# Layer boundaries of a ten-layer float32 kernel: norms in halves, low parts and transposes in another order

## The chip, the cores and the metric

One core of one Trainium2 chip. The metric is device time in microseconds of one execution. TensorE (PE in the rows) does matmuls and transposes, VectorE (DVE) and ScalarE (ACT) do elementwise work, GpSimd (POOL) small roots and masks, SyncE (SP) issues the loads.

## What is computed

256 tokens of width 1024, all in float32. First one block: a SwiGLU layer, a hybrid mixer of three attention kinds, a SwiGLU layer, each with `x = layer_norm(alpha * x + f * layer(x))`. Then a second block with pre-norm residual layers, `x = x + layer(rmsnorm(x, g))`: SwiGLU, a short convolution, SwiGLU, then keys and values that later layers share, SwiGLU, sparse attention (NSA), SwiGLU. The kernel calls these ten layers phases 0 to 9: FFN, MIXER, FFN, FFN, CONV, FFN, KV, FFN, NSA, FFN. The norms between them are

```python
layer_norm: (xf - mu) * rsqrt(var + 1e-5) * g + b
rmsnorm:    xf * rsqrt(mean(xf * xf) + 1e-6) * g
```

Boundary n is what lies between phase n and phase n + 1. Boundaries 0 and 1 have a LayerNorm, boundary 2 a LayerNorm and then an RMS norm, 3 to 8 an RMS norm alone. Boundary 5 leads into KV; the norm of boundary 6 is computed inside KV, which adds nothing to x.

## The kernel before

**Weights** arrive as slabs of 128 x 2048 floats, some narrower (`raw`, six slots), in the order in which they are used. SyncE loads slab k when slab k - 6 is used (`slab_used`). ScalarE rounds a slab to its high part (`split`, L646, `w_hi`), VectorE subtracts to get the low part (`split`, L1016, `w_lo`); `split_to(k)` on either engine does all slabs up to k that are not done. A product is three groups of matmuls: high x high and activation-low x weight-high, which need `w_hi`, and activation-high x weight-low, which needs `w_lo`. Activations are split in the same way.

**Input of a phase.** The 256 tokens are two tiles (`tt` = 0, 1) of 128. When a tile is normed, TensorE turns it (`transpose_input`, L1601) by two quarters of four 128 x 128 transposes, ScalarE copies a quarter out (`xT_hi`, L660), VectorE subtracts the low part (`xT_lo`, L1030). `next_input(n, tt)` on TensorE waits for the norm of a tile and turns both quarters. The operand is x_sb for phases 1 and 2 and z_sb (the RMS norm's output) from phase 3 on.

**End of a phase.** `project` does the last matrix slab by slab into four PSUM banks, one for each tile and half of 512 columns. The last three slabs (four at boundary 2, `tail`) are done for tile 0 first and then for tile 1, so that tile 0's output is complete (`y_ready`) while tile 1's slabs run. Each slab and tile is one `part`: four matmuls of 128 x 512 in each of three groups (L1626, L1629, L1633). `next_input(n + 1, 0)` stands ahead of the last part of tile 1.

**Start of a phase.** In `by_token` the first four slabs (two in phase 0, three in KV) are done for tile 0, then for tile 1; `next_input(n, 1)` stands ahead of slab 2 after an RMS norm alone and ahead of slab 3 after a LayerNorm. `token_slab` (L1694, L1697, L1700) does one slab's three groups.

**The norm, engine by engine.** VectorE's `boundary` adds the output to x in two halves of 512 columns (L1046, L1049). For a LayerNorm it takes the statistics (L1056 to L1059), waits for GpSimd's power of -0.5 (`root`, L590), subtracts the mean and multiplies by the gain (L1067), multiplies by the root and adds the bias (L1069). For an RMS norm ScalarE squares the row of 1024 and sums it (`norm`, L671), VectorE scales and adds epsilon (L1074), GpSimd takes the root, VectorE multiplies by root and gain (L1078). Then the turned input is evacuated (`evacuate_input`).

**Order of the work around the norm.** VectorE: low parts up to slab 2 of the next phase (slab 1 at boundary 2), tile 0's norm and copy; tile 1's addition; then low parts up to slab 3 between its steps (after the LayerNorm's statistics, where boundary 2 stops at slab 2 and does slab 3 ahead of the RMS norm; without a LayerNorm right after the addition), its norm and copy. ScalarE: high parts up to slab 2 (1), tile 0's square and copy, high parts up to slab 3, tile 1's square and copy. Each engine works strictly in the order written by hand; all waits are on semaphores.

In KV, VectorE runs low parts, small clears, the two RMS norms of the next phase's input, a norm of keys and then `xc_lo` (L1359), which the matmuls of L2027 wait for.

## Time and profile before

| | us |
|---|---|
| median of three runs | 1700.6 (1693.1 to 1703.9) |
| the profiled execution, its own time | 1695.3 |
| span of its instructions | 1693.5 |
| TensorE busy | 1647.3 (97%) |
| VectorE busy | 1027.8 (61%) |
| ScalarE busy | 804.6 (48%) |

Loads bring 291 MB at 172 GB/s on average. The span runs from the first to the last instruction of the profiled execution; its own time holds what lies around it, 1.8 us. Busy is the union of an engine's instruction spans; a matmul's end is modelled and spans overlap, so busy TensorE is not TensorE at its peak. The "granted clock" is the share of TensorE's full clock that it was given.

### The profile page before, as it was taken

The page shows a single profiled execution, that of the slowest core. Times are in us where ns is not written, and L with a number is a line of the kernel's source. Part 1 is how long each engine was busy: PE and PEld are TensorE (multiplying, and loading weights), DVE is VectorE, ACT ScalarE, POOL GpSimd, SP SyncE. Part 2 cuts the span into 40 slices and gives each one's busy share as a digit, 9 for nine tenths or more (in the row PEclk, how much of TensorE's full clock was granted, in tenths as well). Part 3 has the DMA queues.
Part 4 walks back from the last instruction along what each step waited for, and adds up shares of the span by engine and source line. Part 5 has one row for each costly group of instructions (what it writes and reads, how often), then busy time and mean ns, then how long its engine had stood idle before and what let it go on. Part 6 is the DMA issues. An engine that isn't in the chain of part 4 may idle for free.

```text
span 1693.5 us, 21209 instructions
## 1 busy us (share of the span) xinstructions
PE 1647.3 (97%) x8854; PEld 1413.7 (83%) x8854; DVE 1027.8 (61%) x1172; ACT 804.6 (48%) x1066; POOL 32.6 (2%) x53
## 2 busy tenths in 40 slices
PE   8999999998999998999999999999999989999998
PEld 6888898866788887888898888889888877888887
DVE  5666565866756656665557566567666444556662
ACT  5555344655355533455334455456455333545551
POOL 0000000000000000000000000000000020000000
PEclk9999999989999999999999999999999986999999
DMA  8565474423556645665565565557565540037552
GB/s 275 179 220 199 137 261 137 137 93 118 174 187 186 236 149 174 199 200 187 173 211 169 180 198 197 190 194 219 174 206 182 172 167 1 2 120 223 184 195 75
DMA packets 226096, 291.23 MB, mean 172 GB/s; under 512 B 10516, under 2 KB 203728, under 8 KB 225872
## 3 DMA queue, kind: packets, MB, share of 16 engines
q1 hardware_dynamic: 226000, 289.87, 52.4%
q8 instruction: 70, 1.15, 0.3%
q14 instruction: 26, 0.21, 0.0%
HBM read 288.78 MB, written 1.05 MB: 171 GB/s over the span
## 4 chain that ended last, share of the span: by engine, by line
PE 84%; DVE 8%; ACT 3%; issue 2%; DMA 2%; POOL 1%; SPq 0%; DVEq 0%; POOLq 0%; ACTq 0%
PE bank L1771 22%; PE bank L1776 12%; PE bank L1626 6%; PE bank L1633 6%; PE bank L1629 6%; PE bank L1694 5%; PE bank L1697 5%; PE bank L1700 5%; DVE w_lo L1016 2%; PE bank L1668 2%; PE bank L1670 2%; PE bank L1675 2%; PE bank L2087 2%; PE bank L1601 1%; PE bank L2112 1%
## 5 line engine op out<-in xcount | busy, mean ns | idle before, releaser
L1016 DVE TENSOR_TENSOR w_lo<-raw,w_hi 128x2048 fp32r<-128x2048 f32 (+1 forms) x268 | 602.4, 2271 | 197.4 <-ACT w_hi L646 196.4
L646 ACT ACTIVATE w_hi<-raw 128x2048 fp32r<-128x2048 f32 (+1 forms) x268 | 508.8, 1904 | 187.3 <-DMA raw<-in_ffn_w_down_dram 92.9
L1771 PE MATMUL bank<-xT,w_hi 128*128 128x512 f32 x1664 | 397.3, 391 | 0.0
L1771 PEld LDWEIGHTS bank<-xT,w_hi 128*128 128x128 f32 x1664 | 306.1, 188 | 59.6
L1776 PEld LDWEIGHTS bank<-xT,w_lo 128*128 128x128 f32 x1664 | 213.3, 191 | 8.1
L1776 PE MATMUL bank<-xT,w_lo 128*128 128x256 f32 x1664 | 215.9, 283 | 0.0
L963 ACT ACTIVATE silu<-bank 128x256 f32<-128x256 f32 x104 | 34.2, 381 | 215.6 <-PE bank L1776 215.6
L1626 PE MATMUL bank<-w_hi,hT_hi 128*128 128x512 f32 x528 | 134.2, 390 | 0.0
L1629 PE MATMUL bank<-w_hi,hT_lo 128*128 128x512 f32 x528 | 133.5, 389 | 0.0
L1633 PE MATMUL bank<-w_lo,hT_hi 128*128 128x512 f32 x528 | 133.5, 389 | 0.0
L1694 PE MATMUL bank<-w_hi,xT 128*128 128x512 f32 (+2 forms) x464 | 126.2, 404 | 6.7 <-ACT w_hi L646 4.0
L1697 PE MATMUL bank<-w_hi,xT 128*128 128x512 f32 (+2 forms) x464 | 119.4, 388 | 0.0
L1700 PE MATMUL bank<-w_lo,xT 128*128 128x512 f32 (+2 forms) x464 | 118.5, 386 | 0.0
L1629 PEld LDWEIGHTS bank<-w_hi,hT_lo 128*128 128x128 f32 x528 | 99.1, 188 | 20.7
L1633 PEld LDWEIGHTS bank<-w_lo,hT_hi 128*128 128x128 f32 x528 | 99.1, 188 | 20.6
L1626 PEld LDWEIGHTS bank<-w_hi,hT_hi 128*128 128x128 f32 x528 | 98.4, 188 | 19.9
L1694 PEld LDWEIGHTS bank<-w_hi,xT 128*128 128x128 f32 x464 | 87.0, 196 | 25.1 <-issue 6.1
L1697 PEld LDWEIGHTS bank<-w_hi,xT 128*128 128x128 f32 x464 | 87.2, 190 | 17.8
L1700 PEld LDWEIGHTS bank<-w_lo,xT 128*128 128x128 f32 x464 | 86.7, 189 | 17.3
L1540 DVE TENSOR_TENSOR h<-silu,h 128x512 f32<-128x512 f32 x52 | 36.0, 693 | 96.4 <-ACT silu L969 96.4
L1535 DVE TENSOR_TENSOR silu<-bank,silu 128x256 f32<-128x256 f32 x104 | 39.3, 419 | 70.7 <-ACT silu L963 70.7
L1668 PE MATMUL bank<-xT,w_hi 128*128 128x256 f32 x304 | 76.0, 289 | 0.0
(268 smaller groups left out, 1592.4 us busy)
## 6 DMA issues: line engine op xcount, KB each, us to landing
raw<-in_ffn_w_gate_up_dram SPq DMA_DIRECT2D x176, 512.0 KB, 4.8
raw<-in_ffn_w_down_dram SPq DMA_DIRECT2D x132, 512.0 KB, 4.1
raw<-in_ffn_w_gate_dram SPq DMA_DIRECT2D x44, 512.0 KB, 4.0
raw<-in_ffn_w_up_dram SPq DMA_DIRECT2D x44, 512.0 KB, 5.1
raw<-in_w_in_dram SPq DMA_DIRECT2D x44, 512.0 KB, 4.9
raw<-in_conv_w_in_dram SPq DMA_DIRECT2D x24, 512.0 KB, 4.7
raw<-in_kv_w_dram SPq DMA_DIRECT2D x12, 512.0 KB, 4.4
raw<-in_w_out_dram SPq DMA_DIRECT2D x8, 512.0 KB, 3.9
```

The lines of the kernel that those rows point to most:

```text
L646: nc.scalar.activation(w_hi[:, slot, 0:width], raw[:, slot, 0:width], ACT.Copy).then_inc(high_ready, 1)
L1016: nc.vector.tensor_tensor(w_lo[:, slot, 0:width], raw[:, slot, 0:width], w_hi[:, slot, 0:width].bitcast(F32), ALU.subtract).then_inc(low_r ...
L1535: ins = nc.vector.tensor_tensor(part[:, fb % 2, :], FEATURES[j % 2][fb][:, 0:S], part[:, fb % 2, :], ALU.add)
L1626: nc.tensor.matmul(o, lhs_hi[:, 2 * d + c, toks], hi[:, c, at], start=d == 0 and c == 0, stop=False, skip_group_check=True)
L1629: nc.tensor.matmul(o, lhs_lo[:, 2 * d + c, toks], hi[:, c, at], start=False, stop=False, skip_group_check=True)
L1633: ins = nc.tensor.matmul(o, lhs_hi[:, 2 * d + c, toks], lo[:, c, at], start=False, stop=d == slabs - 1 and c == 1, skip_group_check=True)
L1668: nc.tensor.matmul(o, hi[:, c, at], xT_hi[:, 4 * kh + c, :], start=kh == 0 and c == 0 and fb % 2 == 0, stop=False, skip_group_check=True)
L1694: nc.tensor.matmul(dst(tt), xT_hi[:, 4 * kh + c, toks], hi[:, c, at], start=kh == 0 and c == 0 and not (shared and tt), stop=False, skip_g ...
L1697: nc.tensor.matmul(dst(tt), xT_lo[:, 4 * kh + c, toks], hi[:, c, at], start=False, stop=False, skip_group_check=True)
L1700: ins = nc.tensor.matmul(dst(tt), xT_hi[:, 4 * kh + c, toks], lo[:, c, at], start=False, stop=kh == 1 and c == 3, skip_group_check=True)
L1771: nc.tensor.matmul(o[:], hi[:, c, at], x, start=kh == 0 and c == 0, stop=False, skip_group_check=True)
L1776: ins = nc.tensor.matmul(o[:, 0:S], lo[:, c, at], xT_hi[:, 4 * kh + c, :], start=False, stop=kh == 1 and c == 3, skip_group_check=True)
```

## The change

- `row_half` and `input_half` are new semaphores. They tell that the first 512 columns of a tile of x are added (or layer-normed), and that the first 512 columns of the next input are ready.
- ScalarE squares each tile in two halves with two sums, the first as soon as `row_half` allows; VectorE combines the sums with one more small operation.
- VectorE applies a LayerNorm's centring before it waits for the root, and its scaling in two halves; the RMS norm's product too is in two halves.
- VectorE's low parts: before tile 0's norm up to slab 2 at boundaries 0 and 1, else up to slab 1. None between tile 1's addition and the end of its norm. Behind the norm and ahead of tile 1's copy: slab 3 at boundaries 0 and 1, slab 2 at 3, 4, 5, 7, 8, none at boundary 2; the rest up to slab 3 behind the copy.
- ScalarE's high part of slab 3 moves from ahead of tile 1's square to behind it where there is no LayerNorm.
- TensorE turns quarter by quarter, each behind its own wait. `next_input(n + 1, 0)` moves from ahead of the last part of tile 1 into it, behind six of its twelve matmuls.
- Phase 3 (behind boundary 2) has its own order: for tile 0 slabs 0 and 1, then the two groups of slabs 2 and 3 that need only high parts, with tile 1's transposes between the last two groups; the same for tile 1 with the hidden layer's transposes (`hidden(0)`) between; then the low groups of slabs 2 and 3 for both tiles.

The diff, cut to what the text speaks of:

```diff
                     for tt in tiles:
-                        if has_ln(n):
-                            act.wait_ge(normed, normed_at(n, tt, LN))
-                        else:
-                            act.wait_ge(summed, summed_before(n) + (tt + 1 if kind != KV else 0))
-                        nc.scalar.activation(z_sb[:, tt, :], x_sb[:, tt, :], ACT.Square,
-                                             accum_out=stats[:, 8 + tt:9 + tt]).then_inc(squared, 1)
+                        for half in range(2):
+                            if phases[n] == KV:
+                                act.wait_ge(summed, summed_before(n))
+                            elif half == 0:
+                                act.wait_ge(row_half, rows_before[n] + tt + 1)
+                            elif has_ln(n):
+                                act.wait_ge(normed, normed_at(n, tt, LN))
+                            else:
+                                act.wait_ge(summed, summed_before(n) + tt + 1)
+                            at, total = slice(half * 512, (half + 1) * 512), (8, 14)[half] + tt
+                            nc.scalar.activation(z_sb[:, tt, at], x_sb[:, tt, at], ACT.Square,
+                                                 accum_out=stats[:, total:total + 1]).then_inc(squared, 1)
...
                         norm(n, [tt])
+                        if tt == 1:
+                            split_to(first_slab[n + 1] + 3)
                         evacuate_input(inputs_before(n + 1), TOKENS_FIRST[2 * tt:2 * tt + 2], 2 * tt)
-                        if tt == 0:
+                        if tt == 0 and has_ln(n):
                             split_to(first_slab[n + 1] + 3)
...
+                        if half == 0 and has_rms(n):
+                            ins.then_inc(row_half, 1)
...
                 xt, mean, rstd = x_sb[:, tt, :], stats[:, 4 * tt:4 * tt + 1], stats[:, 4 * tt + 3:4 * tt + 4]
-                dve.wait_ge(rstd_ready, normed_at(n, tt, LN))
                 dve.wait_ge(gain_loaded[0], 16 * (ln_uses[n] + 1))
...
                                                     op0=ALU.subtract, op1=ALU.mult))
-                nc.vector.scalar_tensor_tensor(out=xt, in0=xt, scalar=rstd, in1=gain[:, 1, :],
-                                               op0=ALU.mult, op1=ALU.add).then_inc(normed, 1)
+                dve.wait_ge(rstd_ready, normed_at(n, tt, LN))
+                first_half = row_half if has_rms(n) else input_half
+                for half, done in enumerate((first_half, normed)):
+                    at = slice(half * 512, (half + 1) * 512)
+                    nc.vector.scalar_tensor_tensor(out=x_sb[:, tt, at], in0=x_sb[:, tt, at], scalar=rstd, in1=gain[:, 1, at],
+                                                   op0=ALU.mult, op1=ALU.add).then_inc(done, 1)
             def rms_norm(n, tt):
-                dve.wait_ge(squared, NT * rms_uses[n] + tt + 1)
-                nc.vector.tensor_scalar(stats[:, 10 + 2 * tt:11 + 2 * tt], stats[:, 8 + tt:9 + tt], 1.0 / D, RMS_EPS,
-                                        ALU.mult, ALU.add).then_inc(spread, 1)
+                mean = stats[:, 10 + 2 * tt:11 + 2 * tt]
+                for half in range(2):
+                    dve.wait_ge(squared, 2 * (NT * rms_uses[n] + tt) + half + 1)
+                    if half == 0:
+                        step(nc.vector.tensor_scalar(mean, stats[:, 8 + tt:9 + tt], 1.0 / D, RMS_EPS, ALU.mult, ALU.add))
+                    else:
+                        nc.vector.scalar_tensor_tensor(out=mean, in0=stats[:, 14 + tt:15 + tt], scalar=1.0 / D, in1=mean,
+                                                       op0=ALU.mult, op1=ALU.add).then_inc(spread, 1)
                 dve.wait_ge(rstd_ready, normed_at(n, tt, RMS))
                 dve.wait_ge(gain_loaded[2], 16 * (rms_uses[n] + 1))
-                nc.vector.scalar_tensor_tensor(out=z_sb[:, tt, :], in0=x_sb[:, tt, :], scalar=stats[:, 11 + 2 * tt:12 + 2 * tt],
-                                               in1=gain[:, 2, :], op0=ALU.mult, op1=ALU.mult).then_inc(normed, 1)
+                for half, done in enumerate((input_half, normed)):
+                    at = slice(half * 512, (half + 1) * 512)
+                    nc.vector.scalar_tensor_tensor(out=z_sb[:, tt, at], in0=x_sb[:, tt, at], scalar=stats[:, 11 + 2 * tt:12 + 2 * tt],
+                                                   in1=gain[:, 2, at], op0=ALU.mult, op1=ALU.mult).then_inc(done, 1)
             def boundary(n, factor, y_at):
-                split_to(first_slab[n + 1] + 5 - tail(n))
+                split_to(first_slab[n + 1] + (2 if has_ln(n) and not has_rms(n) else 1))
                 for tt in range(NT):
...
                         layer_norm(n, tt, factor)
-                        if tt == 1:
-                            split_to(first_slab[n + 1] + (2 if has_rms(n) else 3))
                         layer_norm_apply(n, tt)
+                    if has_rms(n):
+                        rms_norm(n, tt)
+                    if tt == 1 and not (has_ln(n) and has_rms(n)):
+                        split_to(first_slab[n + 1] + (3 if has_ln(n) else 2))
+                    if n < last:
+                        evacuate_input(inputs_before(n + 1), TOKENS_FIRST[2 * tt:2 * tt + 2], 2 * tt)
                     if tt == 1:
                         split_to(first_slab[n + 1] + 3)
-                    if has_rms(n):
-                        rms_norm(n, tt)
-                    if n < last:
-                        evacuate_input(inputs_before(n + 1), TOKENS_FIRST[2 * tt:2 * tt + 2], 2 * tt)
...
                 else:
+                    pe.wait_ge(input_half, NT * (n - 1) + tt + 1)
+                transpose_input(operand(n), TOKENS_FIRST[2 * tt:2 * tt + 1])
+                if n > 0:
                     pe.wait_ge(normed, normed_at(n - 1, tt))
-                transpose_input(operand(n), TOKENS_FIRST[2 * tt:2 * tt + 2])
+                transpose_input(operand(n), TOKENS_FIRST[2 * tt + 1:2 * tt + 2])
...
                                          skip_group_check=True)
-                    for c, toks, at, o in each:
+                    for i, (c, toks, at, o) in enumerate(each):
+                        if between and i == len(each) // 2:
+                            between()
                         nc.tensor.matmul(o, lhs_lo[:, 2 * d + c, toks], hi[:, c, at], start=False, stop=False, skip_group_check=True)
...
+                        between = None
...
-                            next_input(n + 1, 0)
-                        ins = part(d, [tt], tt == 1)
+                            between = lambda: next_input(n + 1, 0)
+                        ins = part(d, [tt], tt == 1, between)
...
+                if between:
+                    between()
...
+            def slab_low(k, kh, width, at, dst, tiles=range(NT)):
...
+                hi, lo = slab_view(k % SLOTS, 4, width)
...
-                for c, tt, toks in each:
-                    ins = nc.tensor.matmul(dst(tt), xT_hi[:, 4 * kh + c, toks], lo[:, c, at], start=False, stop=kh == 1 and c == 3,
-                                           skip_group_check=True)
+                for c in range(4):
+                    for tt in tiles:
+                        ins = nc.tensor.matmul(dst(tt), xT_hi[:, 4 * kh + c, tt * P:(tt + 1) * P], lo[:, c, at], start=False,
+                                               stop=kh == 1 and c == 3, skip_group_check=True)
...
+            def token_slab(k, kh, width, at, dst, shared=False, tiles=range(NT)):
...
+                slab_high(k, kh, width, at, dst, shared, tiles)
+                return slab_low(k, kh, width, at, dst, tiles)
...
                         tile(1)
+                    elif has_ln(n - 1) and has_rms(n - 1):
+                        def high(kh, tt, between=None):
+                            slab_high(s0 + 2 + kh, kh, 512, slice(0, 512), lambda tt: bank[2 + tt][:], tiles=[tt], between=between)
+
+                        for tt in range(NT):
+                            for kh in range(2):
+                                pe.wait_ge(xT_ready, 4 * inputs_before(n) + 2 * tt + kh + 1)
+                                gate_up(0, kh, [tt])
+                            high(0, tt)
+                            if tt == 0:
+                                high(1, 0, lambda: next_input(n, 1))
+                            else:
+                                hidden(0)
+                                high(1, 1)
+                        for kh in range(2):
+                            slab_low(s0 + 2 + kh, kh, 512, slice(0, 512), lambda tt: bank[2 + tt][:]).then_inc(slab_used, 1)
                     else:
```

## Rows read from the trace of the kernel before

**Rows 1.** The page: each engine's busy time.

```profile
PE 1647.3 (97%) x8854; PEld 1413.7 (83%) x8854; DVE 1027.8 (61%) x1172; ACT 804.6 (48%) x1066; POOL 32.6 (2%) x53
```

**Rows 2.** Waits of the whole span, transposes: us, times, longest us.

```profile
PE bank L1601 <- DVE z_sb L1078: 8.9, 12, 4.4
```

**Rows 3.** The groups by line: busy us, mean ns, idle us before.

```profile
L1601 PE MATMUL bank<-ident,x_sb 128*128 128x128 f32 x48 | 7.9, 322 | 7.7 <-DMA x_sb<-in_x_dram 4.3 <-DVE x_sb L1069 3.4
```

**Rows 4.** Timeline, boundary 1, first token tile: start us, duration us, engine.

```profile
451.40 0.55 POOL L590 TENSOR_TENSOR stats<-stats,minus_half 128x1 f32<-128x1 f32 x1 [241.92 <-DVE stats L1059]
...
451.98 1.28 DVE L1067 SCALAR_TENSOR_TENSOR x_sb<-x_sb,stats,gain 128x1024 f32<-128x1024 f32 x1 [0.67 <-POOL stats L590]
...
453.30 1.28 DVE L1069 SCALAR_TENSOR_TENSOR x_sb<-x_sb,stats,gain 128x1024 f32<-128x1024 f32 x1
...
454.64 1.09 PE L1601 MATMUL bank<-ident,x_sb 128*128 128x128 f32 x8 [1.88 <-DVE x_sb L1069]
...
455.97 1.29 DVE L1030 TENSOR_TENSOR xT<-bank,xT 128x512 fp32r<-128x512 f32 x2 [1.38 <-ACT xT L660]
...
458.34 1.07 PE L1694 MATMUL bank<-w_hi,xT 128*128 128x512 f32 x4
```

**Rows 5.** The timeline, boundary 2 (LayerNorm and RMS norm), second token tile.

```profile
645.12 1.07 PE L1694 MATMUL bank<-w_hi,xT 128*128 128x512 f32 x4
...
648.28 2.28 DVE L1016 TENSOR_TENSOR w_lo<-raw,w_hi 128x2048 fp32r<-128x2048 f32 x1
648.44 2.53 POOL L590 TENSOR_TENSOR stats<-stats,minus_half 128x1 f32<-128x1 f32 x1 [8.38 <-DVE stats L1059]
...
653.52 2.29 DVE L1016 TENSOR_TENSOR w_lo<-raw,w_hi 128x2048 fp32r<-128x2048 f32 x1
...
654.61 0.19 ACT L671 ACTIVATION_READ_ACCUMULATOR z_sb<-x_sb 128x1 f32 x1
...
657.88 1.97 PE L1601 MATMUL bank<-ident,z_sb 128*128 128x128 f32 x8 [4.43 <-DVE z_sb L1078]
...
659.50 2.05 PE L1694 MATMUL bank<-w_hi,xT 128*128 128x512 f32 x4
...
663.91 1.07 PE L1694 MATMUL bank<-w_hi,xT 128*128 128x512 f32 x4
```

**Rows 6.** Windows of boundaries 1 and 2: five engines busy us, then granted clock.

```profile
452.00:468.00 16.00, 13.89 (x69) 11.17 (x68) 11.54 (x13) 3.31 (x4) 2.54 (x1) 1.00 0.59 192
658.00:661.00 3.00, 3.00 (x12) 2.71 (x13) 1.18 (x2) 1.72 (x3) 0.00 (x0) 0.50 0.02 5
```

**Rows 7.** The timeline, boundary 4 (convolution to feed-forward), both token tiles.

```profile
924.74 1.06 ACT L671 ACTIVATE z_sb<-x_sb 128x1024 f32<-128x1024 f32 x1 [3.56 <-DVE x_sb L1049]
...
928.08 1.09 PE L1601 MATMUL bank<-ident,z_sb 128*128 128x128 f32 x8 [0.86 <-DVE z_sb L1078]
...
933.17 2.28 DVE L1016 TENSOR_TENSOR w_lo<-raw,w_hi 128x2048 fp32r<-128x2048 f32 x1
...
937.52 1.09 PE L1601 MATMUL bank<-ident,z_sb 128*128 128x128 f32 x8 [0.16 <-DVE z_sb L1078]
```

**Rows 8.** The timeline: transposes on TensorE that waited for nothing.

```profile
1485.53 1.07 PE L1633 MATMUL bank<-w_lo,xT 128*128 128x512 f32 x4
...
1486.44 1.03 PE L1601 MATMUL bank<-ident,z_sb 128*128 128x128 f32 x8
...
1487.23 1.17 PE L1626 MATMUL bank<-w_hi,xT 128*128 128x512 f32 x4
...
1490.05 1.07 PE L1626 MATMUL bank<-w_hi,xT 128*128 128x512 f32 x4
```

**Rows 9.** The timeline of the shared keys' layer, VectorE and then TensorE.

```profile
1142.17 6.69 DVE L1016 TENSOR_TENSOR w_lo<-raw,w_hi 128x2048 fp32r<-128x2048 f32 x3
1149.12 5.72 DVE L1359 TENSOR_TENSOR xc_lo<-bank,xc_hi 64x512 fp32r<-64x512 f32 x8 [0.27 <-ACT xc_hi L863]
...
1152.70 0.39 PE L2027 MATMUL bank<-w_hi,xc_hi 128*80 128x256 f32 x1
```

7 lines of the change are left out of this document (5 added, 2 removed).

## Prediction

> **What bounds the kernel now.** I read the page first. TensorE is busy for 1647.3 of 1693.5 us, VectorE for 61% and ScalarE for 48% [rows 1]: the time is TensorE's own work plus what it waits for. So I then read the waits and the groups by line for the transposes that the change moves (L1601). They follow a norm, and TensorE stood idle before them for 8.9 us in 12 waits where they read z_sb [rows 2] and for 3.4 us where they read x_sb (the 4.3 us behind the load of x are the program's start) [rows 3]. These are two waits at each of eight boundaries (0 to 5, 7, 8), 16 in all, 12.3 us together; boundary 6 lies inside the shared-key layer and has none. Last the timelines. At boundary 1 the chain is statistics, GpSimd's root, centring (L1067), scaling (L1069), transposes, and TensorE has nothing else to do for 1.88 us [rows 4]. At boundary 2 a second norm follows, low parts of weights (L1016) stand between its steps, and TensorE waits 4.43 us [rows 5]. In that wait its granted clock fell: 0.50 in the window from 658 to 661 us, which is the 1.2 GHz level, against 1.00 (2.4 GHz) around boundary 1 [rows 6].
>
> **What the waits cost in all.** (a) Idle: 12.3 us. (b) A matmul group's span overlaps the next group: where transposes waited for nothing they began 0.91 us after the start of the group before, whose span is 1.07 us [rows 8]. A wait loses this overlap too: 0.16 us x 16 = 2.6 us. (c) From eight transposes to the end of the twelve matmuls behind them it took 1490.05 - 1486.44 = 3.61 us without a wait [rows 8] and 458.34 - 454.64 = 3.70 us with one [rows 4]: 0.09 x 16 = 1.4 us. (d) At the low clock the same work at boundary 2 took 663.91 - 657.88 = 6.03 us [rows 5] instead of 3.70: 2.3 us. Sum 18.6 us: the most that can be had.
>
> **Edit 1, transposes of the first tile inside the last slab.** TensorE now has six more matmuls ahead of the wait: 6 x 0.227 (0.91 us for four) = 1.4 us. Behind the transposes six remain to cover the copy of the turned input. L1030 starts 455.97 - 454.64 = 1.33 us behind the first transpose and its first half takes 0.65 [rows 4], so the next layer can begin at 2.0 to 2.1 us; transposes take 0.79 us and six of the twelve matmuls behind them half of 2.82 [rows 8], 2.2 us together. The cover holds by 0.1 to 0.2 us. If it is missed, it costs that much at eight boundaries, about 1 us.
>
> **Edit 2, norms by halves.** Scaling in halves lets the first four transposes start after 0.65 us instead of 1.28. The squares: ScalarE's 1.06 us plus 0.19 for reading the sum [rows 5, 7] become two of about 0.6 + 0.19, the first under the second half of the addition, so the sum is ready about 0.5 us earlier; VectorE gets one more small operation per tile (no row has its own length; 0.1 to 0.3, I take 0.2 with its step). An RMS norm is thus ready 1.1 us earlier. With the 1.4 us of edit 1, all first-tile waits of 0.2 to 1.9 us go. Second-tile waits outside boundary 2 are short, [rows 7] shows one of 0.16 us; there a whole low part (2.28 us) stood beside the square and ended about 1 us after it, and it goes too. These waits end.
>
> **Edit 3, centring before the root is awaited.** Before, the low part L1016 ran beside GpSimd's root and the root took 2.53 us instead of 0.55, ending at 650.97, 0.41 us after the low part [rows 4, 5]. Now the centring, also with two operands in SBUF, runs beside it. Between no conflict (scaling at once behind the centring's 1.28 us, 0.67 us won) and the same conflict (0.41 us later, 0.2 us won) I take the conflict, the nearest row. It matters only where the chain is late, at boundary 2: 0.4 us.
> The Trainium skill, SBUF — State Buffer, section Who interferes with whom, says that a VectorE instruction with two SBUF inputs holds up a GpSimd instruction that reads SBUF until it is finished. By it the conflict is certain and speaks against this edit; without it the sum would be 0.4 us better.
>
> **Boundary 2, second tile.** Count from S, the start of the next layer's first matmul (645.12 before). The root began at S + 3.32 [rows 5]; the addition and statistics ahead of it now end at S + 3.45 (0.2 later than before, since the copy of the first tile is still on VectorE); centring to 4.75, root to 5.2, first half scaled 5.85, second 6.5, second square with its sum 7.45, last statistic 7.7, root 8.35, first half of z 9.05. TensorE is there after two slabs, eight matmuls and four: 36 x 0.227 = 8.2. It waits 1.0 us instead of 4.6. Then three low parts stand ahead of the product that tile 0 of the hidden layer needs (slabs 2, 3 and 4, 2.23 us each in a row [rows 9]): they end about 9.5 us behind the transposes, the product 0.75 later at 10.25, while TensorE, with 4 + 24 + 8 matmuls, asks for it at 9.4: 0.85 us of new wait. With 0.15 for the second half of the transposes, 2.0 us remain here.
>
> **Edit 4, low parts leave the norm.** At boundaries 3, 4, 5, 7, 8 the low parts of slabs 2 and 3 now follow the second tile's norm. From S: z done at 4.9, slab 2's low part to 7.15, the turned copy to 8.4, slab 3's to 10.7. TensorE needs that at 5.44 + 0.79 + 2.82 + 1.81 = 10.86: covered, by 0.15 us. In the convolution and the NSA layer VectorE is idle soon after. In the shared-key layer it isn't. VectorE runs almost without a pause until L1359, whose fourth of eight pieces (5.72 / 2 = 2.86) ends at 1151.98, and TensorE needs it at 1152.70 [rows 9]: 0.72 us of slack. The moved low part brings 2.2 us to this chain, two extra small operations 0.4, the idle 0.27 absorbs some, and TensorE arrives 0.4 earlier for the waits it has lost: 2.2 + 0.4 - 0.27 + 0.4 - 0.72 = 2.0, with its overlap 2.1 us of new wait. Bounds: 0 (if slack I don't see absorbs it) and 2.6. At boundaries 0 and 1 one low part moves behind the norm, ahead of a copy that comes 3 us later: nothing.
> Each load (SyncE) waits for the same slab to be used as before; slabs 2 and 3 of layer 3 are released in the same order, none later. ScalarE's high part of slab 3 moves behind the second square, 9 us ahead of need. Nothing.
>
> **The sum.** 18.6 - 2.0 - 2.1 = 14.5 us. The profiled execution took 1695.3 us, so it would take 1680.8; the median of the runs shown is 1700.6, 0.3% above it, and the forecast is 1700.6 - 14.5 = 1686 us, 0.86% faster. A measurement of this kernel can tell about 1% from no change, so this counts as within 1%.
>
> **Rivals.**
> A, more comes: VectorE has hidden slack in the shared-key layer and in layer 3, no new wait arises: 1700.6 - 18.6 = 1682 us. For it: several short gaps of VectorE there. Against: the chain of [rows 9], with only 0.27 us of waiting ahead of L1359.
> B, the new waits throw the clock down: two waits of about 2 us (shared keys) and 1.0 and 0.85 us close together (boundary 2), each at the price of (d): 14.5 - 4.6 = 9.9, 1691 us. For it: 4.43 us did so. Against: 1.88 us at boundary 1 did not.
> C, the change doesn't bring what it says: TensorE arrives earlier and waits for weights instead (arrival or high part), since loads start only as slabs are released: 1700 us. Against: TensorE shows hardly any wait for w_hi, and VectorE and ScalarE have 39% and 52% free.
> D, slower: the low parts behind the norm come late. The mechanism: slabs 2 and 3 are both converted in the last 6 us before their use at boundaries 3, 4, 5, 7, 8; if both were exposed, 4.5 us each, with the clock falling as at boundary 2 (2.3 us), 5 x 6.8 = 34 us, less 14.5: 1720 us. It decides from the point where slab 3's low part comes about 2.9 us too late (5 x 2.9 = 14.5); I have it 0.15 us early. Against: that needs an error of a whole low part in my count.
>
> **Numbers.** Forecast 0.50 (its own range 1683 to 1689), A 0.25, B 0.12, C 0.09, D 0.04. Range 1679 to 1692: from the whole 18.6 us with 3 us of scatter to B's price; it leaves out C and D and the outer ends. Faster by over 1% is below 1683.6: most of A (0.19) and the lower tail of the forecast (0.12), 0.31; slower by over 1%: D, 0.04; within 1%: 0.65.
>
> **What would show it.** Idle before L1601 under 2 us in all; at boundary 2 one wait near 1.0 us for z and one near 0.85 for h, no fall of the granted clock; the root after LayerNorm near 1.6 us, ending 0.4 us behind the centring; in the shared-key layer a wait of about 2 us before the matmuls on xc. Wrong if the first slab behind each boundary waits for the turned copy, if slab 3's third group waits for w_lo, or if waits for w_hi appear.

## The result, and the profile after

The changed kernel took 1679.24 us (median of 4 runs, 1678.27 to 1681.10), the kernel before in the same comparison 1697.47 us (4 runs, 1693.1 to 1703.9). The ratio is 0.990, with an interval of 0.988 to 0.993. A second comparison, in five rounds, gave 1680.84 against 1696.81 us: 0.992 (0.990 to 0.994). The forecast was 1686 us, a ratio of 0.991, in a range of 1679 to 1692; the first median lies 0.24 us above the range's low end. The profiled execution took 1678.59 us with a span of 1676.9, against 1695.26 and 1693.5: 16.6 us less in the span.

The page of the changed kernel, each engine's busy time; it answers to [rows 1]:

```profile
PE 1642.5 (98%) x8854; PEld 1412.5 (84%) x8854; DVE 1031.0 (61%) x1206; ACT 806.0 (48%) x1094; POOL 34.7 (2%) x53
```

TensorE has the same 8854 matmuls. VectorE has 34 instructions more and ScalarE 28, for 3.2 and 1.4 us more of busy time: halves cost little on engines that are not the bound.

The waits of the changed kernel (us in all, times, longest); the third row answers to [rows 2]:

```profile
PE bank L1625 <- DMA x_sb<-in_x_dram: 4.3, 1, 4.3
...
PE bank L2085 <- DVE xc_lo L1383: 1.6, 1, 1.6
...
PE bank L1625 <- DVE z_sb L1102: 0.6, 1, 0.6
...
PE bank L1801 <- DVE h L1581: 0.4, 1, 0.4
```

Line numbers have moved: the transposes are L1625 (before L1601), the low parts L1028 (L1016), the low part of the shared keys' columns L1383 (L1359) and its user L2085 (L2027). The first row is the load of x at the program's start, as before. Of the 12 waits for z_sb, 8.9 us, one of 0.6 us is left; the group for x_sb shows none on a norm at all, where [rows 3] had 3.4 us. The last row (the hidden layer's product) and the second (the shared keys) are new waits, both foretold.

Boundary 1, first token tile, of the changed kernel; it answers to [rows 4]. Timeline: start us, duration us, engine. PEld is the weight load, which for a transpose is what waits first:

```profile
446.18 1.28 DVE L1080 SCALAR_TENSOR_TENSOR x_sb<-x_sb,stats,gain 128x1024 f32<-128x1024 f32 x1
446.33 1.54 POOL L594 TENSOR_TENSOR stats<-stats,minus_half 128x1 f32<-128x1 f32 x1 [240.10 <-DVE stats L1073]
...
447.99 1.42 DVE L1086 SCALAR_TENSOR_TENSOR x_sb<-x_sb,stats,gain 128x512 f32<-128x512 f32 x2 [0.52 <-POOL stats L594]
...
448.44 0.62 PE L1658 MATMUL bank<-w_hi,xT 128*128 128x512 f32 x2
448.79 0.46 PEld L1625 LDWEIGHTS bank<-ident,x_sb 128*128 128x128 f32 x4 [0.16 <-DVE x_sb L1086]
448.90 1.22 PE L1625 MATMUL bank<-ident,x_sb 128*128 128x128 f32 x8
449.45 0.42 PEld L1625 LDWEIGHTS bank<-ident,x_sb 128*128 128x128 f32 x4 [0.20 <-DVE x_sb L1086]
...
450.16 1.31 DVE L1042 TENSOR_TENSOR xT<-bank,xT 128x512 fp32r<-128x512 f32 x2 [0.76 <-ACT xT L664]
...
450.41 1.09 PE L1662 MATMUL bank<-w_lo,xT 128*128 128x512 f32 x4
...
451.33 1.07 PE L1724 MATMUL bank<-w_hi,xT 128*128 128x512 f32 x4
```

The root now begins with the centring and takes 1.54 us instead of 0.55. The scaling is one row of two pieces, and the transposes start 0.91 us after its start; in [rows 4] it was 1.34 us. TensorE works up to 449.06, so its row shows no wait; only the weight loads waited 0.16 and 0.20 us. The six matmuls behind the transposes reach to the next layer's first matmul (L1724), which has no wait either: the cover of the first tile's copy held, here and at the other seven boundaries.

Boundary 2, second token tile; it answers to [rows 5], with S = 635.88 (the first L1724 of the layer):

```profile
635.88 1.07 PE L1724 MATMUL bank<-w_hi,xT 128*128 128x512 f32 x4
...
639.21 1.55 POOL L594 TENSOR_TENSOR stats<-stats,minus_half 128x1 f32<-128x1 f32 x1 [7.06 <-DVE stats L1073]
...
643.13 1.07 PE L1724 MATMUL bank<-w_hi,xT 128*128 128x512 f32 x4
...
643.98 1.41 DVE L1102 SCALAR_TENSOR_TENSOR z_sb<-x_sb,stats,gain 128x512 f32<-128x512 f32 x2 [0.66 <-POOL stats L594]
...
644.79 1.32 PE L1625 MATMUL bank<-ident,z_sb 128*128 128x128 f32 x8 [0.59 <-DVE z_sb L1102]
...
646.85 0.76 PEld L1724 LDWEIGHTS bank<-w_hi,xT 128*128 128x128 f32 x4 [0.26 <-DVE xT L1042]
...
647.38 6.69 DVE L1028 TENSOR_TENSOR w_lo<-raw,w_hi 128x2048 fp32r<-128x2048 f32 x3
...
653.98 0.75 DVE L1581 TENSOR_TENSOR h<-silu,bank 128x256 f32<-128x256 f32 x2
...
654.78 0.66 PE L1801 MATMUL bank<-ident,h 128*128 128x128 f32 x4 [0.38 <-DVE h L1581]
```

The wait of 4.43 us is now 0.59. A small wait that was not foretold stands behind the transposes: a weight load waits 0.26 us for the turned copy of the second tile. Then come the row of three low parts (6.69 us), and the product L1581 right behind them: TensorE waits 0.38 us for it.

The shared keys' layer, VectorE and then TensorE; it answers to [rows 9]:

```profile
1127.18 6.69 DVE L1028 TENSOR_TENSOR w_lo<-raw,w_hi 128x2048 fp32r<-128x2048 f32 x3
1133.79 5.72 DVE L1383 TENSOR_TENSOR xc_lo<-bank,xc_hi 64x512 fp32r<-64x512 f32 x8
...
1136.68 0.41 PE L2085 MATMUL bank<-w_hi,xc_hi 128*80 128x256 f32 x1 [1.61 <-DVE xc_lo L1383]
```

The fourth of the eight pieces ends at 1133.79 + 2.86 = 1136.65, and TensorE starts 0.03 us later, after 1.61 us of waiting. In [rows 9] it came 0.72 us after that piece's end.

Windows of the changed kernel (busy us of PE, PEld, DVE, ACT, POOL, then the granted clock), at boundary 1, in the wait of boundary 2, and behind the wait of the shared keys:

```profile
444.00:460.00 16.00, 16.00 (x78) 13.15 (x77) 13.86 (x20) 3.00 (x3) 3.10 (x2) 1.00 0.62 198
644.00:647.00 3.00, 2.41 (x14) 1.63 (x14) 2.28 (x4) 1.46 (x3) 0.00 (x0) 1.00 0.00 0
...
1136.00:1140.00 4.00, 3.32 (x20) 3.32 (x21) 3.84 (x6) 3.62 (x7) 0.00 (x0) 0.81 0.71 239
```

Boundary 2 no longer loses the clock (0.50 in [rows 6], 1.00 now, 2.4 GHz). The shared keys' layer now does: a piece of this window ran at 1.2 GHz.

**Where the 16.7 us come from.** Matmuls are the same in number and order outside the changed places, so the start of the same TensorE instruction can be compared between two traces (each has 8854 matmuls). The differences of each stretch, in us gained (the forecast is that of the text, its terms (a) to (d) split by boundary, less the 2.0 us kept at boundary 2):

| stretch | forecast | measured |
|---|---|---|
| boundary 0 | 1.8 | 1.72 |
| boundary 1 | 2.6 | 2.37 |
| boundary 2 | 6.8 | 7.11 |
| boundaries 3, 4, 5 | 0.9, 1.5, 1.1 | 0.83, 1.47, 1.02 |
| shared keys' layer | -2.1 | -2.99 |
| boundaries 7, 8 | 1.0, 0.9 | 0.95, 0.81 |
| **sum of these** | **14.5** | **13.3** |
| program's start, up to boundary 0 | 0 | 1.56 |
| inside the mixer, near 250 us and near 350 us | 0 | 1.26, 0.54 |

The last two have no part of the change in them. The experiments show what is known of them.

### The profile page after: what moved, and what is told of

The parts are those of the page before. It is cut to its first block, busy times and chain, and to the rows that moved or that the text cites. A ratio compares the mean times of both kernels' runs of the same rounds, so it can differ in the third digit from the quotient of the medians.

```text
span 1676.9 us, 21287 instructions
## 1 busy us (share of the span) xinstructions
PE 1642.5 (98%) x8854; PEld 1412.5 (84%) x8854; DVE 1031.0 (61%) x1206; ACT 806.0 (48%) x1094; POOL 34.7 (2%) x53
## 4 chain that ended last, share of the span: by engine, by line
PE 89%; DVE 6%; ACT 2%; DMA 1%; issue 1%; POOL 1%; SPq 0%; DVEq 0%; ACTq 0%
PE bank L1813 23%; PE bank L1818 12%; PE bank L1653 8%; PE bank L1658 8%; PE bank L1662 8%; PE bank L1724 5%; PE bank L1737 5%; PE bank L1729 5%; DVE w_lo L1028 2%; PE bank L2145 2%; PE bank L1698 1%; PE bank L1705 1%; PE bank L1700 1%; PE bank L2170 1%; PE bank L1625 1%
## 5 line engine op out<-in xcount | busy, mean ns | idle before, releaser
L1028 DVE TENSOR_TENSOR w_lo<-raw,w_hi 128x2048 fp32r<-128x2048 f32 (+1 forms) x268 | 601.9, 2271 | 180.7 <-ACT w_hi L650 179.9
L1724 PE MATMUL bank<-w_hi,xT 128*128 128x512 f32 (+2 forms) x464 | 124.1, 398 | 6.2 <-ACT w_hi L650 3.5
L1724 PEld LDWEIGHTS bank<-w_hi,xT 128*128 128x128 f32 x464 | 85.2, 192 | 24.5 <-issue 5.7
```

The lines of the kernel that those rows point to most:

```text
L1028: nc.vector.tensor_tensor(w_lo[:, slot, 0:width], raw[:, slot, 0:width], w_hi[:, slot, 0:width].bitcast(F32), ALU.subtract).then_inc(low_r ...
L1724: nc.tensor.matmul(dst(tt), xT_hi[:, 4 * kh + c, toks], hi[:, c, at], start=kh == 0 and c == 0 and not (shared and tt), stop=False, skip_g ...
```

## The experiments

My theory: the parts gain by ending waits at the boundaries, and lose by new waits where VectorE has no slack. The rivals are named with each run. Most runs are one time and one trace; since single times scatter with the clock, I read the steps of the trace, by boundary as in the table above. "Before on the same chip" was 1697.36 us for the first four runs, 1695.10 for the next four, and 1696.81 (median of 11) for the last three.

**The kernel before, once more.** No edit.

> The kernel before, unchanged, to see what one execution differs from another in. Theory: what the change gained outside the boundaries (1.6 us in the first 18 us, about 1.5 us near 245 us, both with a low granted clock in the profile of before and less of it in the profile of after) is scatter of the clock, so this execution may show either kind, while the waits before the transposes stay at 12.3 us within 0.2. Rival: those 3 us belong to the change, and this execution repeats the earlier profile of before there: 12 matmuls slow at 15 to 20 us, clock 0.72 in that window, and the low stretch near 245 us.

Measured: 1696.98 us. Each wait at a boundary came back: 9.2 us for z_sb, 3.4 for x_sb, the longest 4.4 and 1.9. Step by step against the first trace of the same kernel: +0.77 at the start, +1.23 near 250 us, -0.24 near 350 us, -1.61 at boundary 1, +0.71 at boundary 2, -0.45 in the feed-forward up to boundary 7, -2.25 in the NSA layer. Two rows of its trace at boundary 1, the first from the timeline and the second a window (columns as above):

```profile
452.90 1.76 PE L1601 MATMUL bank<-ident,x_sb 128*128 128x128 f32 x8 [1.88 <-DVE x_sb L1069]
```

```profile
450.00:460.00 10.00, 8.12 (x33) 6.54 (x32) 5.51 (x7) 2.99 (x3) 0.21 (x1) 0.83 0.64 212
```

The same wait of 1.88 us after which [rows 6] shows a clock of 1.00 this time let it fall: in the window from 450 to 460 us it was 1.00 in the first trace and 0.83 in this one, and eight transposes took 1.76 us instead of 1.09. Behind the wait of 4.43 us at boundary 2 the clock fell in both, for 0.71 us less here.

The rest lies outside the change. Near 250 us the granted clock was 0.91 in the first trace of before (window from 236 to 256 us), and 1.00 in this trace and in that of the changed kernel; of the other traces only that of the turn two matmuls later (below) has 0.91 there too. Near 350 us all traces have a stretch at the low level, and it doesn't lie at the same place of the program in each. At the start the first weights' high part was ready 0.36 us earlier (first matmul on w_hi at 11.44 instead of 11.80 us). The clock doesn't explain the remaining 1.2 us by itself: in the first 30 us it was 0.89 in the first trace of before, 0.94 in the changed kernel's, and 1.00 in this trace, which gained only 0.77 us there. No edit touches these stretches, and the unchanged kernel moves in them by itself.

The trace that serves as before matters inside the table too. Against this second one boundary 1 gives 3.99 us instead of 2.37, boundary 2 gives 6.40 instead of 7.11, and the sum is 14.6 us instead of 13.3. The sum is thus known to about 1.3 us.

**One part alone: the turn inside the last slab**, on the kernel before.

```diff
-                    for c, toks, at, o in each:
+                    for i, (c, toks, at, o) in enumerate(each):
+                        if between and i == len(each) // 2:
+                            between()
...
-                            next_input(n + 1, 0)
-                        ins = part(d, [tt], tt == 1)
+                            between = lambda: next_input(n + 1, 0)
+                        ins = part(d, [tt], tt == 1, between)
```

> The kernel before with the first tile's transposes moved behind six matmuls of the last part, nothing else. Theory (each wait shrinks by the 1.4 us of six matmuls, and six matmuls cover the copy): first-tile waits of at most 0.9 us of idle end at boundaries 0, 3, 4, 5, 7, 8, about 0.6 remains at 1 and 0.3 at 2; second-tile waits stay, with the 4.4 us at boundary 2 and its low clock. About 7 us from the boundaries. Rival (six matmuls don't cover the copy): an equal wait appears before the next phase's first matmul, and less than 4 us is gained.

Measured: 1688.55 us; the boundaries gave 1.19, 1.37, 1.62, 0.48, 1.09, 0.62, 0.58, 0.39 = 7.3 us. The waits:

```profile
PE bank L1601 <- DVE z_sb L1078: 5.5, 7, 4.4
...
PE bank L1601 <- DVE x_sb L1069: 1.1, 3, 0.5
```

The first tile's waits go or shrink to what six matmuls (1.4 us) can't cover: 1.88 becomes 0.53 at boundary 1. The second tile's stay, with 4.44 us at boundary 2. The rival that the cover behind the transposes is missing falls: no first matmul of a layer waited.

**One part alone: norms by halves** (squares, scaling, centring ahead of the root, transposes by quarters), low parts and the turn where they were. The norm's functions are those of the changed kernel; the two places that matter most, against the changed kernel:

```diff
             def boundary(n, factor, y_at):
-                split_to(first_slab[n + 1] + (2 if has_ln(n) and not has_rms(n) else 1))
+                split_to(first_slab[n + 1] + 5 - tail(n))
...
-                            between = lambda: next_input(n + 1, 0)
+                            next_input(n + 1, 0)
```

> The kernel before with the norm in halves, centring before the root and transposes by quarters, but the old place of the transposes and of the low and high parts. Theory: an RMS norm is ready 1.1 us earlier, a LayerNorm 0.8, so first-tile waits end but for 1.0 us at boundary 1 and 0.3 at 0 and 2, second-tile waits end but for 3.3 to 3.8 us at boundary 2, where low parts still stand in the norm, and the clock falls there; 8 to 10 us from the boundaries. Rival (centring takes the shared read side from the root right after the low part): the second tile's root at boundary 2 lasts beyond 3.5 us and nothing is won there.

Measured: 1686.13 us; 1.06, 1.02, 2.32, 0.30, 0.99, 0.71, 0.65, 0.51 = 7.6 us at the boundaries, a little less than the 8 to 10 expected. At boundary 2, from the timeline and the waits:

```profile
641.93 2.28 DVE L1026 TENSOR_TENSOR w_lo<-raw,w_hi 128x2048 fp32r<-128x2048 f32 x1
642.09 2.53 POOL L594 TENSOR_TENSOR stats<-stats,minus_half 128x1 f32<-128x1 f32 x1 [8.06 <-DVE stats L1071]
...
650.79 1.97 PE L1623 MATMUL bank<-ident,z_sb 128*128 128x128 f32 x8 [3.69 <-DVE z_sb L1100]
```

Halves save 0.7 us there, and the low parts between the norm's steps keep 3.7. The root waits for the VectorE instruction that stands beside it, whichever this is (it ends 0.41 us after it), and not for two in a row.

**One part alone: the orders** (low parts and ScalarE's high part out of the norm, phase 3's own order), norm in one piece, the turn where it was:

```diff
-                split_to(first_slab[n + 1] + 5 - tail(n))
+                split_to(first_slab[n + 1] + (2 if has_ln(n) and not has_rms(n) else 1))
...
-                        if tt == 1:
-                            split_to(first_slab[n + 1] + (2 if has_rms(n) else 3))
                         layer_norm_apply(n, tt)
-                    if tt == 1:
-                        split_to(first_slab[n + 1] + 3)
                     if has_rms(n):
                         rms_norm(n, tt)
+                    if tt == 1 and not (has_ln(n) and has_rms(n)):
+                        split_to(first_slab[n + 1] + (3 if has_ln(n) else 2))
```

> The kernel before with only the orders changed: low parts and ScalarE's high part behind the norm, and phase 3's own order on TensorE; whole-row norms, old place of the first tile's transposes. Theory: the 4.4 us at boundary 2 becomes 1.6 to 1.8 us and the clock no longer falls there; first-tile waits at 3, 4, 5, 7, 8 end since a low part no longer holds back the addition, second-tile waits end everywhere else; the shared-key layer gets a new wait before the matmuls on xc of 1.2 to 1.6 us. 7 to 9 us in all; with the two runs beside it about 25 us, more than the whole change gained, because the parts cover the same short waits. Rival (the parts add up): less than 3 us here.

Measured: the boundaries gave 0.51, 0.45, 4.37, 0.88, 1.47, 1.02, 0.95, 0.80 = 10.5 us, the shared keys' layer took 1.43. Waits and one timeline row (boundary 2):

```profile
PE bank L1607 <- DVE z_sb L1084: 3.1, 2, 1.6
...
PE bank L2064 <- DVE xc_lo L1365: 1.2, 1, 1.2
...
PE bank L1780 <- DVE h L1563: 0.3, 1, 0.3
```

```profile
651.63 1.09 PE L1607 MATMUL bank<-ident,z_sb 128*128 128x128 f32 x8 [1.56 <-DVE z_sb L1084]
```

Both new waits of the forecast belong to this part alone, and it takes the wait of boundary 2 from 4.43 to 1.56 us; the clock no longer falls there. Its whole time, 1693.3 us, would have hidden this: 8.13 us were lost late in the NSA layer, in a stretch of low clock where this part edits nothing (more below). The three parts alone give 7.3 + 7.6 + 9.0 = 23.9 us, all together 13.3: at most boundaries each part is enough by itself to end a short wait, and such a wait can be won only once.

**The shared keys' wait, first way: low parts before KV in their old place.** ScalarE's high part of slab 3 goes back to its old place there too; all else as changed.

```diff
             def boundary(n, factor, y_at):
-                split_to(first_slab[n + 1] + (2 if has_ln(n) and not has_rms(n) else 1))
+                into_kv = phases[n + 1:n + 2] == [KV]
+                split_to(first_slab[n + 1] + (2 if has_ln(n) and not has_rms(n) or into_kv else 1))
                 for tt in range(NT):
                     add_output(n, tt, factor, y_at)
+                    if tt == 1 and into_kv:
+                        split_to(first_slab[n + 1] + 3)
```

> The changed kernel with the old order of low and high parts at boundary 5 alone (into the shared-key layer). Theory (the moved low part makes the new wait there): the 1.61 us of idle before the matmuls on xc falls to under 0.3, the granted clock stays at 2.4 GHz behind it, a wait of at most 0.3 us comes back before the transposes of boundary 5; 2.5 to 3 us less between the start of that layer and the next. Rival (the halves' extra small operations or a transfer make it): the wait stays above 1 us.

Measured: the layer's step is -0.03 instead of -2.99, and boundary 5 gives 0.74 instead of 1.02. The wait is gone: L1386 starts at 1135.74, its fourth piece ends at 1138.60, and TensorE comes at 1139.18:

```profile
1135.74 5.71 DVE L1386 TENSOR_TENSOR xc_lo<-bank,xc_hi 64x512 fp32r<-64x512 f32 x8
1139.18 0.39 PE L2088 MATMUL bank<-w_hi,xc_hi 128*80 128x256 f32 x1
```

So the order at boundary 5 makes the wait; that it is the low part and not ScalarE's high part, the second way shows, which changes VectorE's queue alone. By steps this version is worth 16.0 us against the changed kernel's 13.3. The whole time is 1684.86 us, above the changed kernel's: this trace lost 2.87 us in the mixer and 1.55 and 3.26 in the NSA layer, where nothing differs, to the clock.

**Second way: three clears behind the low part of the keys.**

```diff
-                    step(nc.vector.memset(v_cmp[:], 0.0))
-                    step(nc.vector.memset(k_cmp[:], 0.0))
-                    step(nc.vector.memset(hid_v[:], 0.0))
                     split_to(s0 + 4)
...
                     split_to(s0 + 9)
+                    step(nc.vector.memset(v_cmp[:], 0.0))
+                    step(nc.vector.memset(k_cmp[:], 0.0))
+                    step(nc.vector.memset(hid_v[:], 0.0))
```

> The changed kernel with the three clears of the shared-key layer (v_cmp, k_cmp, hid_v, 2.4 us of VectorE with their gaps) moved behind the xc_lo pieces. Theory (VectorE's unbroken chain up to xc_lo is what TensorE waits for): the chain is 2.4 us shorter, the 1.61 us wait before the matmuls on xc ends, nothing comes back at boundary 5; 3 us gained with the clock. Rival (ScalarE's xc_hi or a load ends last once VectorE is faster): over 0.5 us of idle remains there.

Measured: step -0.29 instead of -2.99, boundary 5 at 1.02, no wait at L2085 and no fall of the clock behind it. The wait is that of a full queue on VectorE: either piece of work, taken out of it ahead of L1383, ends it. The whole time was 1686.09 us, with 8.09 us lost late in the NSA layer, as in the run with the orders alone.

**Centring behind the root again.**

```diff
+                dve.wait_ge(rstd_ready, normed_at(n, tt, LN))
                 dve.wait_ge(gain_loaded[0], 16 * (ln_uses[n] + 1))
...
                                                     op0=ALU.subtract, op1=ALU.mult))
-                dve.wait_ge(rstd_ready, normed_at(n, tt, LN))
```

> The changed kernel with the LayerNorm's centring behind the wait for the root again. Theory (root and centring compete): the root takes 0.55 us instead of 1.55, yet the scaling starts 0.2 to 0.3 us later, and the wait before the second tile's transposes at boundary 2 grows from 0.59 to about 0.85 us; nothing else moves, since all other waits have slack. Rival (the root's 1.55 us costs the chain its whole excess of 1 us): the wait there shrinks or vanishes.

Measured, boundary 2, timeline:

```profile
640.23 0.55 POOL L594 TENSOR_TENSOR stats<-stats,minus_half 128x1 f32<-128x1 f32 x1 [6.81 <-DVE stats L1073]
...
646.05 1.32 PE L1625 MATMUL bank<-ident,z_sb 128*128 128x128 f32 x8 [0.82 <-DVE z_sb L1102]
```

The root is short again (0.55 us) and the wait is 0.82 instead of 0.59. Boundaries 1 and 2 give 2.13 and 6.86 instead of 2.37 and 7.11 (only boundary 2 was expected to move; at boundary 1 the weight loads wait 0.7 us for x_sb instead of 0.4), boundary 0 gives the same 1.73. Centring ahead of the root is worth 0.25 us at each of these two, though the root triples: the centring's 1.28 us are in the chain in both orders, and what is won is VectorE's wait for a short root (0.67 us in [rows 4]) less the 0.41 us by which the long root outlasts the centring, 0.26. The rival, that the conflict eats it, falls.

**The turn two matmuls later**, four matmuls behind the transposes instead of six.

```diff
-                        if between and i == len(each) // 2:
-                            between()
                         nc.tensor.matmul(o, lhs_lo[:, 2 * d + c, toks], hi[:, c, at], start=False, stop=False, skip_group_check=True)
+                    if between:
+                        between()
```

> The changed kernel with the first tile's transposes behind eight of the twelve matmuls instead of six, so that four remain to cover the copy. Theory (the next phase can begin 2.0 to 2.1 us behind the first transpose; transposes and four matmuls last 1.75): a wait of 0.2 to 0.35 us of idle before the first matmul of each of eight phases, about 3 us in all with the lost overlap. Rival (the cover was never needed, because two quarters are pipelined): no wait and no change.

Measured: the boundaries give 1.35, 2.21, 6.65, 0.53, 1.13, 0.67, 0.61, 0.45, which is 2.7 us less in all. At boundary 1, timeline, weight load and matmul of the next layer's first row:

```profile
453.24 0.76 PEld L1724 LDWEIGHTS bank<-w_hi,xT 128*128 128x128 f32 x4 [0.48 <-DVE xT L1042]
453.24 1.19 PE L1724 MATMUL bank<-w_hi,xT 128*128 128x512 f32 x4
```

The PE row shows no wait. The weight load (PEld) does, 0.48 us, because the last matmul's modelled span reaches over it; the same 0.48 us stands at all eight boundaries. The starts of later instructions give the price: 0.30 to 0.37 us at six of them, 0.46 at boundary 2, and 0.16 at boundary 1, where the weight loads of the transposes waited 0.36 us before and now don't. Whoever reads the PE rows alone misses this. Two matmuls less are 0.45 us less cover and cost about 0.35: the cover of six had 0.1 us to spare.

**The changed kernel, timed in five rounds.**

> The changed kernel, unchanged, in five rounds beside the kernel before. Theory: 13 to 15 us of the gain belong to the boundaries and up to 3 us of the 16.6 between the two profiles was the clock's scatter, so five rounds give 12 to 17 us, ratio 0.990 to 0.993. Rival (the stretches outside the boundaries belong to the change): 17 us or more.

Measured: 1680.84 us (1679.65 to 1689.28, 6 runs), the ratio told above. The profiled execution was the slowest, 1689.28 us. Its median is 16.0 us below that of before, inside the 12 to 17 expected. All boundary steps are those of the table within 0.1 us. The shared keys' step is -1.90 instead of -2.99, though the wait is the same 1.62 us: this time the clock stayed, 1.00 in the window from 1136 to 1146 us where the first trace has 0.83. And 8.08 us were lost late in the NSA layer. Windows of this trace, behind the keys' wait and in the NSA layer:

```profile
1136.00:1146.00 10.00, 8.38 (x56) 7.78 (x55) 9.75 (x11) 7.19 (x11) 0.00 (x0) 1.00 0.50 155
1450.00:1475.00 25.00, 23.23 (x137) 21.97 (x136) 10.80 (x21) 9.32 (x36) 0.00 (x0) 0.73 0.00 1
```

The second of these windows in the changed kernel's first trace:

```profile
1450.00:1475.00 25.00, 23.24 (x160) 20.98 (x159) 11.49 (x21) 10.39 (x28) 0.00 (x0) 1.00 0.12 38
```

TensorE is as busy in both, 23.2 us, but got through 137 matmuls instead of 160 (at a place 2.6 us apart in the program).

**A version that keeps both waits away**: the clears behind the low part, as above, and in phase 3 the product ahead of slab 4's low part (the diff shows the second).

```diff
-                        split_to(s0 + 2 * j + LEAD)
+                        product_first = j == 0 and has_ln(n - 1) and has_rms(n - 1)
+                        if not product_first:
+                            split_to(s0 + 2 * j + LEAD)
```

> The changed kernel with the clears of the shared-key layer behind xc_lo and, in phase 3, the product of the first hidden tile ahead of slab 4's low part. Theory: the 1.61 us wait with its low clock (3.1 us together) and the 0.38 us wait end, nothing comes back: 3 to 4 us below the changed kernel in five rounds; its trace keeps one wait of 0.6 us at boundary 2. Rival (the granted clock takes it back elsewhere, as the single looks at 1684.9 and 1686.1 us suggest): no faster than the changed kernel, with more low clock in the mixer and in the NSA layer in the median of the runs.

Measured: 1677.12 us (1674.31 to 1686.59, 6 runs), ratio to before 0.990 (0.987 to 0.993). The shared keys' step is -0.33, boundary 2 gives 7.69 instead of 7.11. The one wait left of those that this study is about, and the product's place between four low parts, in its timeline:

```profile
647.13 1.32 PE L1627 MATMUL bank<-ident,z_sb 128*128 128x128 f32 x8 [0.59 <-DVE z_sb L1102]
...
649.73 4.48 DVE L1028 TENSOR_TENSOR w_lo<-raw,w_hi 128x2048 fp32r<-128x2048 f32 x2
655.38 0.75 DVE L1583 TENSOR_TENSOR h<-silu,bank 128x256 f32<-128x256 f32 x2 [1.17 <-ACT silu L996]
```

The sum of steps is 16.6 us at boundaries and shared keys against 13.3, and the medians differ by 3.7 us. By their intervals the times alone don't part the two kernels; the traces do.

**Low parts at the boundaries with an RMS norm alone in their old place** (all five, the one into KV included), with ScalarE's high part of slab 3 in its old place there, and the product first:

```diff
             def boundary(n, factor, y_at):
-                split_to(first_slab[n + 1] + (2 if has_ln(n) and not has_rms(n) else 1))
+                split_to(first_slab[n + 1] + 5 - tail(n))
                 for tt in range(NT):
                     add_output(n, tt, factor, y_at)
+                    if tt == 1 and not has_ln(n):
+                        split_to(first_slab[n + 1] + 3)
```

> The changed kernel with the old order of low and high parts at all boundaries with an RMS norm alone (3, 4, 5, 7, 8), and the product first in phase 3. Theory (transposes in the slab and norms in halves alone end the short waits there, as each of them nearly did by itself): no idle over 0.15 us at these boundaries, no wait before the matmuls on xc, within 1 us of the kernel best. Rival (the moved low parts are needed there): waits of 0.15 us or more come back before second-tile transposes.

Measured: 1680.64 us (1677.18 to 1685.89, 6 runs), ratio 0.991 (0.989 to 0.992). Boundaries 3, 4, 5, 7, 8 give 0.59, 1.20, 0.72, 0.70, 0.50 instead of 0.87, 1.49, 1.01, 0.95, 0.81; the shared keys' step is -0.01. Boundary 3, timeline:

```profile
825.10 2.28 DVE L1028 TENSOR_TENSOR w_lo<-raw,w_hi 128x2048 fp32r<-128x2048 f32 x1
...
827.30 0.14 DVE L1094 TENSOR_SCALAR stats<-stats 128x1 f32<-128x1 f32 x1
...
829.11 0.42 PEld L1629 LDWEIGHTS bank<-ident,z_sb 128*128 128x128 f32 x4 [0.25 <-DVE z_sb L1102]
```

One low part between addition and norm holds the sum of squares back until 827.30, and the weight loads of the transposes wait twice 0.25 us. So the theory (no idle over 0.15 us, within 1 us of the version before it) failed, and its rival holds: by steps this version is 1.1 us behind, in the medians 3.5. Moving low parts, with the high part, is worth 0.3 us at each of five boundaries, 1.4 us, and cost 1.9 to 3.0 us in the shared keys' layer. Without the clears moved too, that part of the change loses more than it brings at the boundaries with an RMS norm alone. All of the loss comes from the one place ahead of KV.

## Why the prediction was right, and where it was off

**The whole.** The time lies in the range, 0.24 us above its low end; the ratio, 0.990 and 0.992 in two comparisons, stands on both sides of the forecast's 0.991. In medians the gain was 18.2 and 16.0 us where 14.5 stood. The first of these is flattered: the forecast counted from a median of 1700.6 us, and the kernel before measured 1697.47 beside the changed one; the steps that the change explains came to 13.3 us (14.6 against the second trace of before), and the profiled executions differed by 16.7 because of stretches that the change doesn't touch. Both comparisons have intervals that hold 13.3 us (0.9922). That the ratio came so close, and that the time stayed inside the range, is in part luck.

**The limits of the gain, (a) to (d).** Right as a sum. 16.3 us came at the eight boundaries where 16.6 stood. That waits cost their overlap and a restart beside their idle shows in single terms: at boundary 2 the product's wait shows 0.38 us of idle, and taking it away gave 0.58. Term (d), 2.3 us of low clock at boundary 2, was one execution's: the second trace of before lost 0.71 us less there, and 1.6 us at boundary 1 where the sum had nothing.

**Edit 1.** Right, and closer than it had to be: cover of 0.1 to 0.2 us foretold, 0.1 found with the turn two matmuls later. The price of missing it was 0.30 to 0.37 us at six of the eight boundaries there.

**Edit 2.** Right in its parts: a half square takes 0.63 us and its sum 0.19, the added small operation 0.16.

**Edit 3.** The root took 1.54 to 1.56 us after all six LayerNorm tiles and ended 0.41 us behind the centring; the gain was 0.25 us where 0.2 stood, at boundaries 1 and 2 and not at 2 alone. This is the rule that the Trainium skill gives (SBUF — State Buffer, section Who interferes with whom: a VectorE instruction with two SBUF inputs holds up a GpSimd instruction that reads SBUF until it is finished). The traces agree, and add the 0.41 us by which the held-up root outlasts it. That the rule spoke against the edit was true of the root and not of the chain.

**Boundary 2.** Both waits came, in the places foretold, and the clock stayed. Sizes were off to the good side. For z: 0.59 us of idle and 0.16 of overlap, where 1.0 stood; its first half was ready at S + 8.9 (foretold 9.05), and TensorE ended its 36 matmuls at S + 8.3 (8.2). For the product: 9.9 us behind the transposes instead of 10.25, so 0.38 of idle instead of 0.85. The other side of that wait has a slip: the terms shown for TensorE's arrival, 0.79 and 36 x 0.227 us, add up to 8.96 and not to the 9.4 that stood; the trace has 9.6, with the small waits behind the transposes. Small waits are differences of long chains: the product 0.3 us earlier and TensorE 0.2 us later, 3% and 2% of their chains, took more than half of the 0.85 us.

**Edit 4.** The step that counted: a new wait in the shared keys' layer of 2.1 us with its overlap. The wait was 1.61 us of idle and cost 1.9 us where the clock held. The mechanism (a low part moved into a queue without enough slack) is shown by the two runs that took work out of it.
The term that was mis-sized is the same: it left the clock out. In three of four traces with this wait of 1.6 to 1.7 us the clock fell right behind it, and the step was -2.97 to -3.09 instead of -1.90: 1.1 us more. Rival B had that mechanism, and I gave it both places and 2.3 us each with one chance of 0.12; it came in one place, at half the price. My argument against it, that 1.88 us at boundary 1 had left the clock alone, rested on one execution, and the next trace of the same kernel shows it fall there.

**Rivals.** A (no new wait) fell for the changed kernel; the version without them gained 3.3 us more by steps, against the 4.1 that A had. C fell: no weight was waited for behind a boundary (of the turned copies one was, the second tile's at boundary 2, for 0.26 us), and the one wait for w_hi at the program's start (3.5 us) was there before (4.0). D fell: the third group of slab 3 was covered at all five boundaries.

**What stays open.** Why the clock fell at the same place late in the NSA layer in four of the thirteen traces and not in the others: orders alone, clears late and the changed kernel timed again lost 8.1 us each, low parts before KV early 3.26 us. No edit is there, and the same kernel shows both. Open too is what moves the start by 0.77 us in the unchanged kernel.

## What to carry to other kernels

Add up the waits of one kind before pricing the edits that end them: three edits worth 7, 8 and 9 us alone gave 13 together, because each short wait is won once. When work is moved off one path, follow its engine's queue to the first place without slack, even a layer away: here a low part that left a norm cost 1.9 us some 30 us further on, and three clears that nobody needs until later stood in the same queue. And compare kernels by the starts of the same instruction, stage by stage: the changed kernel's steps at the boundaries came back within 0.1 us while whole times of one kernel moved by 9 to 10 us (1679.65 to 1689.28 us, 1692.61 to 1701.33). Take two traces of the kernel before as well: its step at boundary 1 moved by 1.6 us with the clock.

## What the runs showed of the hardware

- The granted clock is not a function of the program. In two traces of the same kernel, the same wait of 1.88 us left it at 1.00 in one and brought it down in the other (0.83, both in the window from 450 to 460 us). In two traces of the changed kernel a wait of 1.6 us did so in one and not in the other (0.83 and 1.00 in the window from 1136 to 1146 us).
- A stretch at the low level came late in the NSA layer in three traces (0.73 in the window from 1450 to 1475 us of one) and cost 8.1 us each time. That is more than any single boundary of this study, and the slowest of the six times of the changed kernel (1689.28 us, median 1680.84) is an execution that had it. A fourth trace, low parts before KV early, had a shorter one there that cost 3.26 us:

```profile
1461.00:1469.00 8.00, 8.00 (x46) 8.00 (x45) 2.64 (x6) 1.85 (x4) 0.00 (x0) 0.57 0.01 2
```

- The longest stretch at the low level stands in every trace, earlier in the NSA layer, and no part of the change bears on it. These are the windows of the kernel before and of the changed kernel:

```profile
1385.00:1415.00 30.00, 24.89 (x93) 20.17 (x93) 13.47 (x22) 10.00 (x35) 2.19 (x2) 0.50 0.00 1
```

```profile
1370.00:1400.00 30.00, 25.32 (x95) 20.72 (x96) 14.06 (x23) 9.59 (x34) 1.35 (x1) 0.50 0.00 1
```

- A wait can hide from the matmul rows: 0.48 us on the weight load and nothing on the matmul behind it, at eight boundaries, for 2.7 us of time in all.
- GpSimd's root took 0.55 us alone, 1.54 to 1.56 us beside a centring of 1.28 us and 2.53 us beside a low part of 2.28 us, and ended 0.41 us behind either.
